# Second tile's queries moved up, norm moved behind the scores, and ten gather places from the 13th gather on

## The chip, the cores and the metric

The kernel runs on one core of a Trainium2 chip. The metric is the device time of one execution in microseconds; the time of a kernel is the median of its runs. A profiled execution gives the trace. Engines: TensorE (PE), VectorE (DVE), ScalarE (ACT), GpSimd (POOL), and SyncE (SP), which issues most of the DMA transfers.

## What is computed

The program computes two transformer blocks on 256 tokens of width 1024, all in float32. The change lies in the second half of the first block, a feed-forward layer of 16384 single-neuron experts (PEER):

```python
h = h + hybrid_mixer(rmsnorm(h, norm_mix), ...)
h = h + peer_ffn(rmsnorm(h, norm_ffn), peer_wq, peer_subkeys, peer_u, peer_v)

def peer_ffn(h, wq, subkeys, u, v):
    q = (hf @ wq).reshape(T, 8, 2, 128)                   # 8 heads, two half queries
    s = einsum('thpd,hpnd->thpn', q, subkeys)             # 128 keys for each half
    s1, i1 = top_k(s[:, :, 0], 16); s2, i2 = top_k(s[:, :, 1], 16)
    cand = s1[..., :, None] + s2[..., None, :]            # 256 pairs
    top_s, pos = top_k(cand, 16)                          # 16 experts for a token and head
    w = softmax(top_s)
    coef = w * gelu(einsum('cd,chkd->chk', x, u[idx]))
    return einsum('chk,chkd->cd', coef, v[idx])
```

The rmsnorm divides each token by its root mean square and multiplies each column by a gain. A query and a score are linear in their token, so a factor of a token may be applied before the queries or to the scores. The second block (a delta-rule mixer and experts of 2 x 1024) follows.

## The kernel before

The 256 tokens are two tiles (t = 0, 1) of 128 partitions. `merge_and_peer` ends the mixer and does the PEER layer. Five engine programs run side by side; each engine works strictly in the order in which its calls are written, and semaphores (`wait_ge`) tie them. Nothing else sets an order.

**End of the mixer.** `up(t, c, half)` (PE L1136) and `merge` (DVE L1799, L1802) build the merged branches, `project` (PE L1147) multiplies by w_out, `residual` (DVE L1807) adds to h. `squares` (ACT L1509), `mean` (DVE), `root` (ACT L1514) and the reciprocal (DVE L1818) give the inverse root mean square of each token; `scale` (DVE L1821) writes the scaled token, `transposes` (PE L1156) turn it, `evacuate` (ACT L1519 and DVE L1826, four blocks each) bring it to hT with the gains.

**Queries and keys.** There are 8 heads. Heads 0 and 1 have their weights in `first_wq`, heads 2 to 7 come through a ring of four pieces (`late_ring`, SP L83) and are split in a high and a low part (`split_high`, ACT L1549; `split_low`, DVE L1837), as hT is (`parts_high`, ACT L1543; `parts_low`, DVE L1831). `first_queries` (PE L1167) and `first_scores` (L1174) do tile 0 of heads 0 and 1, `second_queries` (L1181) and `second_scores` (L1189) tile 1 of them; `queries` (L1199) and `scores` (L1212) do the other heads for both tiles at once. The keep functions of ACT copy the results out of PSUM (queries L1524, L1533, L1553; scores L1528, L1537, L1557). A unit u is a tile and a head, 16 in all, tile 0 first. `first_level`, `pairs`, `places` and `experts_of` (DVE, from L1847 on) choose the unit's 16 experts, `place_numbers` (PE L1246) and `keep_numbers` (DVE L1894) bring their numbers into the order of the gathers, `weights` (ACT L1562), `share_out`, `place_shares` (PE L1253) and `keep_shares` do the softmax.

**Gathers.** GpSimd issues 256 indirect gathers (L1109), 16 for a unit. Gather n, counted from 0, brings 128 rows of 8 KB (an expert's u and v), so 1 MB. `dots` (DVE L1921) multiplies u with the tokens, `coefficients` (ACT L1642 gelu, L1649 two or four diagonals) and `picks` (PE L1224) add the weighted v. They go in quads j of four gathers; up to quad 11 in two groups of two. When a group's picks are done its places are free (`slot_free`), and a later gather may be issued into them. Sixteen places of 1 MB exist; many hold something else at first. Places 0 to 5 are free early, 6 after the projection of tile 1, 7 and 8 hold `first_wq` and are free after `second_queries` of heads 0 and 1, 9 is hT. The table `phases` says which places take turns from which gather on:

```python
phases = [(0, range(AFTER_OUT - 1)), (12, range(AFTER_OUT)), (26, range(EARLY)), (96, ...), (144, ...)]
```

with AFTER_OUT = 7 and EARLY = 10: six places, seven from gather 12, ten from 26, twelve from 96, eleven from 144. For a place that held something else the issue waits: `out_ps` 4 for place 6, `q0_ps` 3 for 7, `q0_ps` 4 and `h_low` 2 for 8 and 9.

SP copies the normalised tokens of tile 0 to the order of the gathers (16 DMAs, L1066), which the first dot needs.

Of the kernel before, what the change touches and what calls it, by code (L numbers as in the profile page):

```python
# [13 lines left out]
ALU = mybir.AluOpType  # L14
# [898 lines left out]
def merge_and_peer(T):  # L913
# [19 lines left out]
    for j in range(QUADS):  # L933
# [44 lines left out]
    phases = [(0, range(AFTER_OUT - 1)), (12, range(AFTER_OUT)), (26, range(EARLY)), (96, [i for i in range(OVER_ROWS) if i not in (AT_ONCE, AT_ONCE + 1)]),  # L978
              (144, [i for i in range(len(slot_of)) if i not in (AT_ONCE, AT_ONCE + 1, EARLY - 1, EARLY, EARLY + 1)])]
# [7 lines left out]
    for n in range(PICKS):  # L987
# [20 lines left out]
    squares_done, mean_done, root_done, scaled, bank_ready, h_act, h_dve, h_high, h_low = (sem(f"ffn_{n}") for n in (  # L1008
        "squares", "mean", "root", "scaled", "bank_ready", "h_act", "h_dve", "h_high", "h_low"))
# [41 lines left out]
    with nc.Block() as block:  # L1051
        @block.sync
        def _(sync):
# [6 lines left out]
            sync.wait_ge(up_ps, 5)  # L1060
            for u in range(4, 6):
                late_ring.issue(sync, u - 4, T.stream1(G_WQ + u))
            sync.wait_ge(row_ready, 1)
            for g in range(4):
                for k in range(4):
                    sync.dma_start(rows_at[0][32 * k:32 * (k + 1), g, :], token_rows[0][32 * g:32 * (g + 1), :]).then_inc(first_rows, 16)  # L1066
            sync.wait_ge(up_ps, 6)
# [59 lines left out]
        def _(pe):  # L1127
# [24 lines left out]
            def transposes(t):  # L1152
                for b in range(2):
                    pe.wait_ge(scaled, 2 * t + b + 1)
                    for k in range(4):
                        last = nc.tensor.transpose(ps[:, 2 * t + b, k * P:(k + 1) * P], xs[:, t, (4 * b + k) * P:(4 * b + k + 1) * P],  # L1156
                                                   ident[:, :])
                    last.then_inc(bank_ready, 1)
# [19 lines left out]
            def second_queries(hd):  # L1178
                for c in range(2):
# [5 lines left out]
            def second_scores(hd):  # L1185
                pe.wait_ge(q_sb, (4, 6)[hd])
# [18 lines left out]
            def scores(hd):  # L1205
                pe.wait_ge(q_sb, {2: 3, 3: 5}.get(hd, hd + 3))
# [178 lines left out]
            project(0)  # L1385
            up(1, 0, 0)
            up(1, 0, 1)
            transposes(0)
# [24 lines left out]
            for j in range(2, QUADS):  # L1413
                if j == 2:
                    picks(2, slice(0, 1))
                    transposes(1)
                    place_shares(1)
                    picks(2, slice(1, 2))
                elif j == 3:
                    picks(3, slice(0, 1))  # L1420
                    pe.wait_ge(h_low, 2)
                    queries(4)
                    queries(5)
                    picks(3, slice(1, 2))
# [13 lines left out]
                if j == 4:  # L1438
                    scores(2)
                    queries(6)  # L1440
                    second_queries(0)
                if j == 5:
                    scores(3)
                if j == 6:
                    second_scores(0)
                    second_queries(1)
# [49 lines left out]
        def _(act):  # L1496
# [38 lines left out]
            def second_keep_scores(hd):  # L1535
                act.wait_ge(sc_ps, hd + 5)
                nc.scalar.activation(sc[:, 1, 2 * hd:2 * hd + 2, :], ps[:, 2 + hd, 0:2 * NKEYS].rearrange("p (c k) -> p c k", c=2),  # L1537
                                     ACT.Copy).then_inc(sc_sb, 1)
# [16 lines left out]
            def keep_scores(hd):  # L1555
                act.wait_ge(sc_ps, hd + 1 if hd < 4 else hd + 3)
                nc.scalar.activation(sc[:, :, 2 * hd:2 * hd + 2, :], ps[:, 2 + hd % 2, :].rearrange("p (t c k) -> p t c k", t=NT, c=2),  # L1557
                                     ACT.Copy).then_inc(sc_sb, 1)
# [100 lines left out]
            squares(0, 0)  # L1659
            squares(0, 1)  # L1660
            root(0)
            evacuate(0)
# [7 lines left out]
            squares(1, 0)  # L1670
            coefficients(2)
            squares(1, 1)
            root(1)
            act.wait_ge(out_ps, 2 * NT)
# [1500 lines left out]
```

## Time and profile before

| | us |
|---|---|
| median of 3 runs | 2092.22 (2092.11 to 2095.01) |
| profiled execution | 2084.8 |
| its span (first to last instruction) | 2083.0 |
| PE busy | 1383.6 (66%) |
| DVE busy | 753.2 (36%) |
| ACT busy | 421.1 (20%) |
| POOL busy | 414.6 (20%) |
| DMA, mean of the whole | 355 GB/s |

Times in the text are microseconds from the start of the span. The gathers run from 250.7 to about 932. The profile splits the span in 40 slices of 52 us and gives the DMA's share for each; the same can be had for any stretch. A share slightly above 1 is rounding of the packets' times and means a full DMA.

### The profile page before, as it was taken

The numbers are of one execution on the slowest core, as the hardware profiler recorded it, in microseconds if no ns is written. First come the engines' busy times: TensorE is split into PE (matmuls) and PEld (weight loads), VectorE is DVE, ScalarE is ACT, GpSimd is POOL, SyncE is SP. The second block draws the span as 40 slices with busy tenths as digits, with TensorE's granted clock in tenths as the row PEclk, the third lists the DMA queues.
The fourth block names the chain that finished last, engine by engine and source line by source line (L and its number), as shares of the span: only waits on it lengthen the run. The fifth ranks groups of instructions, "written<-read, shape, count | busy, mean of one in ns | idle before, by whom it ended". The sixth has DMA issues, their size and how long they took to land. (4 is left out here: it accounts for less than half of the span.)

```text
span 2083.0 us, 24370 instructions
## 1 busy us (share of the span) xinstructions
PE 1383.6 (66%) x9429; PEld 614.3 (29%) x9429; DVE 753.2 (36%) x1687; ACT 421.1 (20%) x1005; POOL 414.6 (20%) x353
## 2 busy tenths in 40 slices
PE   7998967655443333358988876666666676666665
PEld 7887934322010000016887211011111110111111
DVE  4565466677777767646653100000000000000001
ACT  4456132222223211216532100000000000000001
POOL 0141134444444444424540000000000000000000
PEclk9999988877656655579999988777788777777877
DMA  7534579999999999996226899999999999999997
GB/s 269 179 126 166 165 283 380 419 421 420 398 419 421 420 420 420 420 385 251 79 86 247 356 420 420 420 421 420 420 421 420 420 421 421 420 420 420 420 420 324
DMA packets 110711, 739.43 MB, mean 355 GB/s; under 512 B 13472, under 2 KB 14752, under 8 KB 26656
## 3 DMA queue, kind: packets, MB, share of 16 engines
q1 hardware_dynamic: 73472, 469.71, 55.8%
q0 software_dynamic: 36864, 268.45, 31.3%
q8 instruction: 58, 0.95, 0.2%
q14 instruction: 29, 0.24, 0.0%
q10 hardware_dynamic: 288, 0.08, 0.0%
HBM read 735.05 MB, written 1.05 MB: 353 GB/s over the span
## 5 line engine op out<-in xcount | busy, mean ns | idle before, releaser
L2807 PE MATMUL ps<-arena,xe 128*32 128x512 f32 x2016 | 367.4, 821 | 185.1 <-DMA arena<-in_experts_in 184.3
L1224 PE MATMUL ps<-arena 128*32 128x512 f32 x768 | 245.6, 948 | 292.7 <-ACT arena L1649 292.7
L2987 DVE TENSOR_TENSOR low<-low,ps 128x512 f32<-128x512 f32 x16 | 11.0, 688 | 878.3 <-PE ps L2807 878.3
L1109 POOL DMA_INDIRECT arena<-in_peer,arena x192 | 223.9, 1166 | 387.2 <-PE ps L1224 270.9
L1921 DVE CUSTOM_DVE_ANT_0 arena<-arena 128x1024 f32<-128x1024 f32 x192 | 233.1, 1224 | 118.2 <-DMA arena<-in_peer,arena 117.6
L2835 PE MATMUL ps<-arena,hT 128*32 128x512 f32 x1024 | 161.5, 733 | 82.0 <-DMA arena<-in_experts_down 70.9
L3019 POOL TENSOR_TENSOR low<-h,hT 128x512 f32<-128x512 f32 x2 | 2.5, 1264 | 993.2 <-DVE h L3003 993.2
L2807 PEld LDWEIGHTS ps<-arena,xe 128*32 128x32 f32 x2016 | 47.3, 123 | 492.9 <-DMA arena<-in_experts_in 464.2
L1224 PEld LDWEIGHTS ps<-arena 128*32 128x32 f32 x768 | 41.0, 147 | 418.2 <-ACT arena L1649 339.6
L1642 ACT ACTIVATE arena<-arena 128x4 f32<-128x4 f32 (+2 forms) x81 | 16.6, 204 | 467.0 <-DVE arena L1921 466.9
L1224 PE MATMUL ps<-peer_slot,arena 128*32 128x512 f32 x100 | 81.1, 960 | 16.6 <-ACT arena L1649 16.6
L2835 PEld LDWEIGHTS ps<-arena,hT 128*32 128x32 f32 x1024 | 25.5, 121 | 201.1 <-DMA arena<-in_experts_down 160.8
L1224 PE MATMUL ps<-ring,arena 128*32 128x512 f32 x112 | 60.2, 1040 | 35.8 <-ACT arena L1649 35.8
L2824 PE MATMUL ps<-low,og 128*128 128x512 f32 x128 | 71.9, 689 | 11.5 <-ACT low L2898 11.5
L2898 ACT ACTIVATE low<-ps 128x512 f32<-128x512 f32 x32 | 19.1, 597 | 262.8 <-PE ps L2835 262.8
L2895 ACT ACTIVATE hT<-ps 128x512 f32<-128x512 f32 x16 | 9.5, 596 | 303.4 <-PE ps L2814 303.4
L2890 ACT ACTIVATE low<-ps 128x512 f32<-128x512 f32 x16 | 9.6, 597 | 283.8 <-PE ps L2807 283.8
L1279 PE MATMUL ps<-first_h_parts,first_w_parts 128*128 128x256 f32 x480 | 63.6, 291 | 2.5 <-ACT first_h_parts L1579 1.9
L1649 ACT ACTIVATE arena<-arena 128x32 f32<-128x32 f32 x256 | 63.1, 311 | 7.9 <-DVE arena L1909 0.4
L1279 PEld LDWEIGHTS ps<-first_h_parts,first_w_parts 128*128 128x128 f32 x480 | 60.1, 196 | 7.6 <-issue 3.5
L1117 POOL TENSOR_TENSOR first_w_parts<-arena,first_w_parts 128x512 fp32r<-128x512 f32 x36 | 49.3, 1385 | 61.7 <-ACT first_w_parts L1586 61.1
L513 PE MATMUL ps<-first_h_parts,first_w_parts 128*128 128x256 f32 x384 | 50.1, 287 | 2.5 <-POOL first_w_parts L481 2.2
(481 smaller groups left out, 2009.1 us busy)
## 6 DMA issues: line engine op xcount, KB each, us to landing
arena<-in_experts_in SPq DMA_DIRECT2D x252, 1024.0 KB, 26.9
arena<-in_experts_down SPq DMA_DIRECT2D x128, 1024.0 KB, 26.9
ring<-in_stream SPq DMA_DIRECT2D x38, 512.0 KB, 4.4
arena<-in_stream SPq DMA_DIRECT2D x32, 512.0 KB, 4.1
arena<-in_stream SPq DMA_DIRECT2D x14, 1024.0 KB, 8.2
first_out_w<-in_stream SPq DMA_DIRECT2D x8, 512.0 KB, 7.3
arena<-in_peer,arena POOLq DMA_INDIRECT x192, 15.0
arena<-arena SPq DMA_DIRECT2D x16, 128.0 KB, 2.4
```

The costliest lines, as they stand in the source:

```text
L513: last = nc.tensor.matmul(ps[:, 7, (u % 2) * S:(u % 2 + 1) * S], w[:, k, :], T.parts[:, x, k, :], start=(k == 0 and m == 0), stop=(k == KB ...
L1109: nc.gpsimd.indirect_dma_start(slot(n), None, A["peer"], bass.IndirectOffsetOnAxis(ap=idx[:, u % 3, k:k + 1], axis=0)).then_inc(landed[pla ...
L1117: nc.gpsimd.tensor_tensor(low, half_raw(u, hk), high.bitcast(F32), ALU.subtract).then_inc(f_low, 1)
L1224: last = nc.tensor.matmul(ps[32 * g:32 * (g + 1), 4 + 2 * t + half, :], diag[:, n % DIAGS, :], slot(n)[:, D + half * BANK:D + (half + 1) * ...
L1279: last = nc.tensor.matmul(ps[:, n % 4, half * S:(half + 1) * S], w[:, k, :], T.parts[:, x, k, :], start=(k == 0 and m == 0), stop=(k == KB ...
L1642: nc.scalar.activation(act_out[:, u % 2, some], act_in[:, u % 2, some], ACT.Gelu).then_inc(gelu_done, 1)
L1649: nc.scalar.activation(diag[:, n % DIAGS, :], shares[:, u % 2, n % TOPK, :], ACT.Copy, scale=act_out[:, u % 2, n % TOPK:n % TOPK + 1]).the ...
L1921: nc.vector.tensor_tensor_reduce(slot(n)[:, 0:D], slot(n)[:, 0:D], rows_at[n // FIRST][:, n % G, :], 1.0, 0.0, ALU.mult, ALU.add, act_in[: ...
L2807: last = nc.tensor.matmul(ps[32 * j:32 * (j + 1), 4 + r // KB, :], xe[:, k, :], w[:, j * BANK:(j + 1) * BANK], start=(k == 0), stop=(k == ...
L2824: last = nc.tensor.matmul(ps[:, 2 * t + half, :], og[:, t * P:(t + 1) * P], yb[:, half * BANK:(half + 1) * BANK], start=opening, stop=clos ...
L2835: last = nc.tensor.matmul(ps[32 * j:32 * (j + 1), 6 + half, :], hidT[:, i, 32 * j:32 * (j + 1)], w[:, j, :], start=(i == 0), stop=(i == 3) ...
L2898: nc.scalar.activation(yb[:, half * BANK:(half + 1) * BANK], ps[:, 6 + half, :], ACT.Copy).then_inc(y_ready, 1)
```

## The change

Five things change together, all in `merge_and_peer`.

1. The transposes read h itself and not the scaled token; `scale` is gone, `invert` keeps only the reciprocal. The factor of the token is applied where ACT copies the scores out of PSUM, for heads 2 to 7 with one copy for each tile instead of one for both.
2. For tile 0 the first half of the transposes goes into the projection, and `up(1, 0, ...)` and `merge(1, 0)` behind the first two heads.
3. SP issues the 16 token copies ahead of weight pieces 4 and 5 instead of behind them.
4. For tile 1 the order of ACT, DVE and PE around quads 1 to 4 is rewritten; `second_queries(0)` and `(1)` follow the transposes in quads 2 and 3, and not in quads 4 and 6.
5. `phases`: ten places from gather 12, twelve from 102, eleven from 138.

```diff
-    phases = [(0, range(AFTER_OUT - 1)), (12, range(AFTER_OUT)), (26, range(EARLY)), (96, [i for i in range(OVER_ROWS) if i not in (AT_ONCE, AT_ONCE + 1)]),
-              (144, [i for i in range(len(slot_of)) if i not in (AT_ONCE, AT_ONCE + 1, EARLY - 1, EARLY, EARLY + 1)])]
+    phases = [(0, range(AFTER_OUT - 1)), (12, range(EARLY)), (102, [i for i in range(OVER_ROWS) if i not in (AT_ONCE, AT_ONCE + 1)]),
+              (138, [i for i in range(len(slot_of)) if i not in (AT_ONCE, AT_ONCE + 1, EARLY - 1, EARLY, EARLY + 1)])]
@@ transposes (PE)
-                    pe.wait_ge(scaled, 2 * t + b + 1)
+                    pe.wait_ge(res_done, 2 * t + b + 1)
@@ second_queries (PE)
+                pe.wait_ge(h_act, 8)
+                pe.wait_ge(h_dve, 8)
@@ PE, tile 0
-            project(0)
-            up(1, 0, 0)
-            up(1, 0, 1)
-            transposes(0)
+            project(0, range(6))
+            transposes(0, range(1))
+            project(0, range(6, 8))
+            transposes(0, range(1, 2))
...
+            up(1, 0, 0)
+            up(1, 0, 1)
             up(1, 1, 0)
+            place_numbers(0)
             up(1, 1, 1)
             up(1, 2, 0)
-            place_numbers(0)
@@ first_keep_scores (ACT; the other two copies of scores likewise)
+                act.wait_ge(rstd, 1)
-                                     ACT.Copy).then_inc(sc_sb, 1)
+                                     ACT.Copy, scale=ssq[:, 10:11]).then_inc(sc_sb, 1)
@@ DVE, tile 1
-            residual(1, 1)
-            mean(1)
-            keep_numbers(1)
-            scale(1)
-            split_low(4)
-            dots(4)
-            share_out(1)
-            evacuate(1)
-            split_low(5)
-            parts_low(0)
-            dots(5)
-            parts_low(1)
+            dots(4)
+            keep_numbers(1)
+            residual(1, 1)
+            dots(5)
+            evacuate(1)
+            parts_low(0)
+            mean(1)
+            share_out(1)
+            dots(6)
+            invert(1)
+            parts_low(1)
+            split_low(4)
+            dots(7)
+            keep_shares(1)
+            split_low(5)
```

**ScalarE, from the coefficients of gathers 4 and 5 to those of 10 and 11.** L1642 is the gelu of a group and L1649 its diagonals, L1509 the squares, L1514 the root, L1562 the softmax's exp, L1549 and L1543 the high parts of weights and of hT. Before:

```order
L1509 ACTIVATE arena,ffn_ss<-h 128x512
L1514 ACT_TABLE_LOAD
L1514 ACTIVATE ffn_ss<-ffn_ss 128x1
L1549 ACTIVATE first_w_parts<-ring1 128x1024
L1642 ACT_TABLE_LOAD
L1642 ACTIVATE arena<-arena 128x2
L1649 ACTIVATE arena<-arena 128x32 x2
L1562 ACT_TABLE_LOAD
L1562 ACTIVATE arena<-arena 128x16
L1543 ACTIVATE first_h_parts<-hT 128x8x128
L1549 ACTIVATE first_w_parts<-ring1 128x1024
```

The first gelu here is that of gathers 6 and 7: squares, root and a weight's split stand ahead of it.

The same place now (gelu L1655, diagonals L1662, squares L1517, root L1522, exp L1575, split of weights L1558, of hT L1552, evacuation L1527, copy of the second tile's queries L1542), from the diagonals of gathers 6 and 7 on:

```order
L1662 ACTIVATE arena<-arena 128x32 x2
L1575 ACT_TABLE_LOAD
L1575 ACTIVATE arena<-arena 128x16
L1655 ACT_TABLE_LOAD
L1655 ACTIVATE arena<-arena 128x2
L1662 ACTIVATE arena<-arena 128x32 x2
L1552 ACTIVATE first_h_parts<-hT 128x8x128
L1517 ACTIVATE arena,ffn_ss<-h 128x512 x2
L1655 ACTIVATE arena<-arena 128x2
L1662 ACTIVATE arena<-arena 128x32 x2
L1527 ACTIVATE hT<-ps,gains 128x128 x4
L1522 ACT_TABLE_LOAD
```

The coefficients of 6 and 7 come first, then exp, those of 8 and 9, the squares, those of 10 and 11, and the root behind them. And on, up to the coefficients of gathers 12 and 13 (second gelu row's L1662) and 14 and 15:

```order
L1542 ACTIVATE arena<-ps 128x2x128
L1552 ACTIVATE first_h_parts<-hT 128x8x128
L1558 ACTIVATE first_w_parts<-ring1 128x1024
L1655 ACT_TABLE_LOAD
L1655 ACTIVATE arena<-arena 128x2
L1662 ACTIVATE arena<-arena 128x32 x2
L1542 ACTIVATE arena<-ps 128x2x128
L1558 ACTIVATE first_w_parts<-ring1 128x1024
L1655 ACTIVATE arena<-arena 128x2
L1662 ACTIVATE arena<-arena 128x32 x2
```

The copies of the second tile's queries (L1542) now stand ahead of both groups' coefficients.

**TensorE, from the second tile's transposes (L1156) on.** Picks are L1224 before and L1226 now, shares L1253 and L1255, queries of heads 2 and on L1199 and L1201. Before:

```order
L1156 MATMUL ps<-ident,arena 128x128 x8
L1253 MATMUL ps<-peer_small 32x16 x4
L1224 MATMUL ps<-arena 32x512 x8
L1199 MATMUL ps<-first_h_parts,first_w_parts 128x256 x48
L1224 MATMUL ps<-arena 32x512
```

Now:

```order
L1156 MATMUL ps<-ident,h 128x128 x8
L1226 MATMUL ps<-arena 32x512 x4
L1183 MATMUL ps<-hT,arena 128x128 x16
L1226 MATMUL ps<-arena 32x512 x4
L1255 MATMUL ps<-peer_small 32x16 x4
L1183 MATMUL ps<-hT,arena 128x128 x16
L1226 MATMUL ps<-arena 32x512
```

The second tile's queries of heads 0 and 1 (L1183) stand between the picks of quads 2 and 3, where before there were picks alone and then the queries of head 2.

## Rows read from the trace of the kernel before

**Rows 1.** The page's second part: DMA share in 40 slices.
```profile
DMA  7534579999999999996226899999999999999997
```

**Rows 2.** Windows: length, busy us of each engine, clock, DMA share, GB/s.
```profile
283.00:292.00 9.00, 3.89 (x10) 0.69 (x12) 4.75 (x9) 8.33 (x14) 1.88 (x2) 0.66 0.22 67
...
302.00:311.00 9.00, 7.73 (x35) 3.27 (x36) 6.20 (x10) 2.12 (x9) 3.25 (x3) 0.77 0.25 75
...
341.00:346.00 5.00, 5.00 (x26) 2.75 (x23) 4.93 (x8) 0.74 (x3) 1.91 (x2) 0.73 0.33 103
346.00:534.00 188.00, 107.43 (x650) 52.52 (x652) 136.75 (x334) 50.01 (x136) 84.66 (x72) 0.78 1.01 417
534.00:538.00 4.00, 1.03 (x8) 0.00 (x0) 3.97 (x9) 0.00 (x0) 2.05 (x3) 0.90 0.60 199
```

**Rows 3.** GpSimd: its waits from 250 to 372, then gathers 11, 12, 16.
```profile
POOL arena L1109 <- PE ps L1224: 60.6, 11, 11.4
...
276.80 1.39 POOL L1109 DMA_INDIRECT arena<-in_peer,arena  x1 [0.30 <-issue]
289.62 0.94 POOL L1109 DMA_INDIRECT arena<-in_peer,arena  x1 [11.44 <-PE ps L1224]
...
307.14 1.86 POOL L1109 DMA_INDIRECT arena<-in_peer,arena  x1 [10.29 <-PE ps L1224]
```

**Rows 4.** Timeline around the holes: start, length, engine, line, idle before and releaser.
```profile
276.14 1.23 DVE L1921 CUSTOM_DVE_ANT_0 arena<-arena 128x1024 f32<-128x1024 f32 x1 [1.15 <-DMA arena<-in_peer,arena]
...
279.81 0.68 DVE L1807 TENSOR_TENSOR h<-h,ps 128x512 f32<-128x512 f32 x1
...
282.67 1.04 ACT L1549 ACTIVATE first_w_parts<-ring 128x1024 fp32r<-128x1024 f32 x1
...
283.73 1.28 ACT L1642 ACT_TABLE_LOAD   x1
...
285.85 3.49 PE L1224 MATMUL ps<-arena 128*32 128x512 f32 x8 [5.64 <-ACT arena L1649]
...
294.32 1.84 PE L1156 MATMUL ps<-ident,arena 128*128 128x128 f32 x8
...
302.79 3.55 PE L1224 MATMUL ps<-arena 128*32 128x512 f32 x8 [6.45 <-ACT arena L1649]
...
334.19 3.73 PE L1181 MATMUL ps<-hT,arena 128*128 128x128 f32 x32
...
340.05 3.46 PE L1224 MATMUL ps<-arena 128*32 128x512 f32 x8 [2.14 <-ACT arena L1649]
```

**Rows 5.** Timeline of the first tile, from its residual to the first gather.
```profile
229.54 0.69 DVE L1807 TENSOR_TENSOR h<-h,ps 128x512 f32<-128x512 f32 x1 [6.46 <-PE ps L1147]
...
232.92 1.04 PE L1156 MATMUL ps<-ident,arena 128*128 128x128 f32 x8
...
234.84 3.81 PE L1167 MATMUL ps<-hT,arena 128*128 128x128 f32 x32 [0.89 <-ACT hT L1519]
...
240.35 0.49 DVE L1847 MAX8 arena<-arena 128x8 f32<-128x128 f32 x2 [2.20 <-ACT arena L1528]
...
250.73 1.15 POOL L1109 DMA_INDIRECT arena<-in_peer,arena  x1 [73.94 <-DVE arena L1894]
```

**Rows 6.** SyncE's issues: weight pieces (L83) and token copies (L1066).
```profile
233.11 0.80 SPq L83 DMA_DIRECT2D ring<-in_stream  x2
...
236.58 10.95 SPq L1066 DMA_DIRECT2D arena<-arena  x16
...
248.26 0.81 SPq L83 DMA_DIRECT2D ring<-in_stream  x2
```

**Rows 7.** Prices: picks at full clock, head 2's first keys, unit 2's numbers.
```profile
306.82 1.91 PE L1224 MATMUL ps<-arena 128*32 128x512 f32 x8 [0.48 <-ACT arena L1649]
...
332.15 0.49 DVE L1847 MAX8 arena<-arena 128x8 f32<-128x128 f32 x2 [6.07 <-ACT arena L1557]
...
349.04 0.17 DVE L1894 CAST arena<-ps 128x16 uint32<-128x16 f32 x1
```

More of the change, by code:

```diff
@@ L1007, in merge_and_peer @@
         "no_ready", "no_ps", "share_ready", "share_ps", "shares", "row_ps", "row_kept", "first_rows"))
-    squares_done, mean_done, root_done, scaled, bank_ready, h_act, h_dve, h_high, h_low = (sem(f"ffn_{n}") for n in (
-        "squares", "mean", "root", "scaled", "bank_ready", "h_act", "h_dve", "h_high", "h_low"))
+    squares_done, mean_done, root_done, rstd, bank_ready, h_act, h_dve, h_high, h_low = (sem(f"ffn_{n}") for n in (
+        "squares", "mean", "root", "rstd", "bank_ready", "h_act", "h_dve", "h_high", "h_low"))
     q0_ps, w_high, w_low, unit_done, q_sb = (sem(f"ffn_{n}") for n in ("q0_ps", "w_high", "w_low", "unit_done", "q_sb"))
@@ L1556, in keep_scores @@
                 act.wait_ge(sc_ps, hd + 1 if hd < 4 else hd + 3)
-                nc.scalar.activation(sc[:, :, 2 * hd:2 * hd + 2, :], ps[:, 2 + hd % 2, :].rearrange("p (t c k) -> p t c k", t=NT, c=2),
-                                     ACT.Copy).then_inc(sc_sb, 1)
+                if hd == 2:
+                    act.wait_ge(rstd, 2)
+                for t in range(NT):
+                    last = nc.scalar.activation(sc[:, t, 2 * hd:2 * hd + 2, :], ps[:, 2 + hd % 2, 2 * t * NKEYS:2 * (t + 1) * NKEYS].rearrange("p (c k) -> p c k", c=2),
+                                                ACT.Copy, scale=ssq[:, 10 + t:11 + t])
+                last.then_inc(sc_sb, 1)
             def weights(u):
@@ L1814, in mean, with invert @@
                                                ALU.mult, ALU.add).then_inc(mean_done, 1)
-            def scale(t):
+            def invert(t):
                 dve.wait_ge(root_done, t + 1)
-                link(nc.vector.reciprocal(ssq[:, 10 + t:11 + t], ssq[:, 8 + t:9 + t]))
-                for b in range(2):
-                    cols = slice(b * BANK, (b + 1) * BANK)
-                    nc.vector.tensor_scalar(xs[:, t, cols], h[:, t, cols], ssq[:, 10 + t:11 + t], None, ALU.mult).then_inc(scaled, 1)
+                nc.vector.reciprocal(ssq[:, 10 + t:11 + t], ssq[:, 8 + t:9 + t]).then_inc(rstd, 1)
+                dve.wait_ge(rstd, t + 1)
             def evacuate(t):
@@ L2052, in _ @@
             residual(0, 1)
+            evacuate(0)
             mean(0)
-            scale(0)
-            evacuate(0)
+            invert(0)
             dve.wait_ge(peer_consts, 32)
-            dve.wait_ge(h_act, 4)
-            dve.wait_ge(h_dve, 4)
             token_row(0)
-            merge(1, 0)
             nc.vector.reduce_sum(stacked[:, :], ident[:, :].rearrange("p (g r) -> p r g", g=4), AX.X)
@@ L2066, in _ @@
             share_out(0)
-            for c in range(1, 4):
+            for c in range(4):
                 merge(1, c)
```

76 lines of the change are left out of this document (40 added, 36 removed).

## The prediction

> **What bounds the kernel now.** I read the page first: its DMA row [rows 1] stands at nine tenths or more from the eighth slice on, and again over the last twenty slices. Two stretches of the program move data as fast as the chip gives it; the first (252 to 928 us) is the 256 gathers, 1 MB each. The windows of equal state [rows 2] show a share of 1.01 where nothing stops them (346 to 534 us at 417 GB/s: 2.5 us for a gather), and four holes. Against a share of 1.00 they are 9 x 0.78 = 7.0 us at 283 to 292, 9 x 0.75 = 6.8 at 302 to 311, 5 x 0.67 = 3.4 at 341 to 346 and 4 x 0.40 = 1.6 at 534 to 538: together 18.8 us. Everything after the last gather waits for it, so the time of the whole moves with the sum of the holes and with the start of the stream, and with nothing else in this stretch. In the undisturbed stretch TensorE is busy for 57%, VectorE for 73 and ScalarE for 27: none of them sets the pace.
>
> Then the queue of the gathers [rows 3]: GpSimd waited 60.6 us for the matmuls of L1224 (they free a place), and its long waits end at 289.62 and 307.14, each after 10 us or more, with the holes in front. So a hole is a late slot: landing, dot (DVE L1921), gelu and two diagonals (ACT), eight matmul halves (PE), then the next gather.
>
> Who is late at each hole [rows 4]. First: gathers 6 and 7 have landed by 276.14 (the dot of 7 stood waiting for it), yet their matmuls start at 285.85, because ScalarE did the second tile's norm (squares for DVE's residual at 279.81, root) and a weight split (282.67) ahead of their coefficients. Second: the matmuls at 302.79 stand behind the transposes of 294.32, their evacuation and the wait of DVE for it. Third: the matmuls at 340.05 stand behind a head's queries (334.19, 3.73 us).
>
> **Start, worked out.** Before, residual (229.54) to first keys (240.35) holds squares, mean, root, two scalings and the transposes [rows 5]. Now the transposes read h at once: the first four go into the projection (0.52 us, half of the 1.04 of the row at 232.92), so the projection ends at 230.0; residual to 230.9; the other four to 231.5; queries 3.81 us to 235.3 instead of 238.65; their evacuation, scores and the scaled copy follow as before, so the first keys start at 237.1, 3.3 us earlier. The rstd is there by 233.9: squares (0.8), mean, root and reciprocal (1.0 together) run beside the queries. From keys to first gather 10.4 us as before, so 247.5 instead of 250.73; TensorE's three halves of `up` put ahead of the numbers end at 246.8, inside that.
>
> But the stream of the weights moves too [rows 6]. Before, SP issued two 512 KB pieces at 233.11, into an idle DMA, then the 16 row copies (10.95 us), then two pieces at 248.26. Now the row copies come first (235.4 to 246.4), and all four pieces, 2 MB, go out from 246.5 to 249.8, at the door of the gathers. That is 1 MB more, 2.5 us. Position of the stream: before, 9 MB (two pieces, eight gathers) stood between 248.26 and gather 7's landing at 276.14; they are 22.5 us of transfer, and 5.4 of delay and gaps. Now 10 MB from 246.5: 25.0 + 5.4 gives 276.9, 0.8 late, less what of the gaps closes now that the gathers are issued at once behind the pieces. **The head start is worth 0** (bounds: 3.2 gained if the pieces fit into gaps, 1 lost). DVE is at its merges until 257.6 anyway, since TensorE's last half of `up` ends at 256.3.
>
> **First hole.** Up to gather 11 all is as before, within 0.3 us. ScalarE goes from the coefficients of gathers 4 and 5 straight to those of 6 and 7: dots done at 277.4, diagonals 278.3; TensorE, behind the numbers of unit 1 (280.3), picks at 280.5 and frees them by 282.4 (1.91 us at 2.4 GHz [rows 7]). Gather 12 is issued at 282.6 and not 289.62, before the queue is dry (284). **Hole gone: 7.0 us.** What is next: gathers 8 and 9 are picked at 283.5 to 285.4, transposes to 286.5, and gather 11, the last landed (286.1 by the pace from 276.14), has its dot at 287.4, coefficients 288.2, picks 290.2. So 12 to 17 are issued on time.
>
> **Second hole, turned into another.** Ten places take turns from gather 12, so 18 and 19 need no freed place: 18 the second tile's projection, 19 the first head's queries (q0_ps 3). 20 and 21 need the second head's queries (q0_ps 4). TensorE does the first head's at 290.2 to 293.9; 19 goes out at 294.3. The DMA is then fed until 284.2 + 8 x 2.5 = 304.2. Chain to gather 20, on ScalarE: root (before 290.9), copy of the queries 0.4, h's high part 1.05, weight split 1.04, gelu table back 1.28, coefficients 0.8: 298.5. On TensorE: picks 3.55 at 1.2 GHz, since it has stood for 4.6 us (the row at 302.79 is such a case), 302.1; shares 0.3; queries 3.7: 306.1. Gather 20 is issued at 306.5 and moves from 307.9: **a hole of 3.7 us**, instead of 6.8. The new waits of TensorE (h_act, h_dve, q_sb) end before and cost nothing; if DVE were 3 us later at 300 they still would not.
>
> **Third hole.** Then, in order: query copy and split to 307.6, coefficients 308.4, picks 310.4, two query units (3.0 each) 316.4, split 318.2, coefficients of 16 and 17 at 319.0, picks 321 (322.6 at 1.2 GHz), head 2's scores and two scaled copies 323 to 324.5. The queue holds 20 to 25 and two pieces of weights: 307.9 + 6 x 2.5 + 2.5 = 325.4, so 26 comes in time; 28 to 31 follow at 326 to 334 and fill until 342. Gather 32 needs unit 2's numbers: before, 16.9 us from its first keys (332.15) to the numbers (349.04), now plus one split (1.2): 324 + 18.1 = 342.1, moving at 343.5. **Hole 1.5 us** (0 to 4) instead of 3.4. From there ten places as before, and the engines are some 8 us earlier but the DMA 12 us: 1 us of small gaps allowed. The keeping of scores is now two copies with a scale for six heads: 0.4 us each on an engine that is a fifth busy.
>
> **Fourth.** The hole at 534 stands where the turn shrinks and a place comes round after 8 gathers while picks go in fours. The later phase (102) has two such gathers, 108 and 109, five behind the end of their quad as before: 1.6 stays. At 145 the distance is six: one gather more of slack, nothing.
>
> **Sum.** Holes before 18.8; after 3.7 + 1.5 + 1.0 + 1.6 = 7.8. Gain 11.0 us, start 0. Profiled execution: span 2083.0 (2084.8 with what lies around it), now 2072. It lies 7 us under the median of the runs, 2092.2, in which the same 11.0 come off: **2081**.
>
> The Trainium skill, ScalarE: Activation LUTs, "What ACT_TABLE_LOAD costs", gives each change of table set a drain of 1.38 us beside the load of 1.28. The trace shows the load alone: 283.73 + 1.28 ends at 285.01, and the coefficients' matmuls begin at 285.85 after a gelu and two copies of 0.8 us in all; no drain fits. By the page two changes (exp to gelu, root to gelu) would lie ahead of gathers 8 and 20, of which the second counts: a hole of 5.1, total 2082.
>
> **Rivals.**
> *Late second head (chance 0.17).* The same mechanism, but TensorE at 1.2 GHz in more of the chain: picks of 10 and 11 at 3.5, both heads' queries at 7.4. For it: 285.85, 302.79 and 340.05 are all at that clock after 2 to 6 us of standing. Against: 306.82 and 334.19 are back at 2.4. One head's queries slow and the picks before them: + 1.6 + 3.7 us, and a split further behind: holes 13 to 15, gain 4 to 6, 2087.
> *The start counts (0.08).* Pieces fit beside the first gathers and the third hole closes: 3 more from the start, 2 from holes: 2076.
> *Slower than before (0.06).* Gathers 20 and 21 stop GpSimd, and with it 22 to 25, whose places are free: the turn of ten makes the stream wait for the second head where a turn of seven would have gone on. With both heads at 1.2 GHz: queries to 299.3, ScalarE 303.9, picks 307.4, queries 315.2, a hole of 12.5 us instead of 3.7; the same delay of some 10 us runs through queries 4 and 5 to gather 26 and on to 32, where the next hole is then 10 or more, and the pieces' 2.5 us at the start are lost. It decides above 19 us of holes: 26, time 2099.
> *It does not arrive (0.04).* The gathers end 11 us earlier, but the later stages give part back: 2092. Against: the loads of the next stage are released by the last gathers; no row shows another clock.
> The forecast has the rest, 0.65, with its own range 2077 to 2085.
>
> **How the numbers follow.** 0.2% is 4.2 us, about what a measurement of this kernel can tell from no change. Faster: 0.65 + 0.08 + two thirds of the late second head (0.11) = 0.84, of which 0.04 goes off for what I have not seen, half to each side: 0.80. Within: 0.06 + 0.04 + 0.02 = 0.12. Slower: 0.06 + 0.02 = 0.08. The range takes in the late second head and the early start: 2075 to 2089.
>
> **What would show it.** Gather 12 issued within a microsecond of 283, no hole at 284. A hole that ends at GpSimd's wait for the second head's queries near 307 (gather 20); 19 issued near 294. First gather at 247.5 but its dots not before 257. Holes in all near 8 us, and the last gather landing 11 us earlier. Wrong would be: a first hole that is still there (ScalarE or the residual late), gather 20 later than 312, or a stream at less than 420 GB/s between the holes.

## The result and the profile after

The changed kernel takes 2079.49 us (median of 5 runs, 2075.34 to 2083.99) against 2092.22 (median of 5 runs, 2091.01 to 2096.52) of the kernel before: a ratio of 0.9934, 95% interval 0.9915 to 0.9953, or 12.7 us less (9.8 to 17.8). The forecast was 2081, range 2075 to 2089. The time is right; the sum behind it is not in all its terms, and this section and the experiments show which.

The profiled execution took 2075.34 us, its span is 2073.6. Beside [rows 1], the page's row of the DMA's share in 40 slices of 52 us:

```profile
DMA  7544599999999999986306899999999999999997
```

Before, the nines begin in the seventh slice (the prediction says the eighth); now they begin in the sixth, 260 to 312 us, where the first two holes lay, and the gathers' row of nines ends a slice sooner. The windows that answer to [rows 2] (length, busy us of PE, PE's weight loads, DVE, ACT and POOL, granted clock of TensorE as a share of 2.4 GHz, DMA share, GB/s):

```profile
283.00:292.00 9.00, 5.62 (x30) 1.85 (x28) 7.09 (x15) 5.62 (x17) 4.25 (x4) 1.00 0.95 366
292.00:302.00 10.00, 5.50 (x40) 3.92 (x38) 7.10 (x15) 5.64 (x9) 3.96 (x4) 0.92 1.00 414
302.00:311.00 9.00, 6.78 (x52) 4.49 (x50) 2.84 (x5) 1.95 (x5) 2.31 (x2) 0.88 0.76 292
311.00:341.00 30.00, 24.04 (x140) 15.24 (x138) 19.99 (x52) 7.76 (x20) 14.13 (x11) 0.89 1.00 410
341.00:346.00 5.00, 2.58 (x24) 1.43 (x22) 4.90 (x13) 4.59 (x8) 1.12 (x2) 1.00 0.97 396
346.00:534.00 188.00, 104.50 (x616) 46.24 (x612) 144.81 (x351) 47.02 (x136) 87.84 (x74) 0.77 1.01 418
...
541.00:547.00 6.00, 3.52 (x28) 0.66 (x20) 3.35 (x6) 2.48 (x3) 3.32 (x3) 0.86 0.79 294
```

A share of 0.22 at 283 has become 0.95, 0.25 at 302 has become 0.76, 0.33 at 341 has become 0.97. The undisturbed stretch moves 418 GB/s, before it was 417. What made the difference, GpSimd's gathers 12, 19, 20 and 32 (start, length, idle before and its releaser; beside [rows 3]):

```profile
284.84 0.94 POOL L1109 DMA_INDIRECT arena<-in_peer,arena  x1 [4.04 <-PE ps L1226]
...
297.51 0.93 POOL L1109 DMA_INDIRECT arena<-in_peer,arena  x1 [0.30 <-issue]
...
308.39 0.94 POOL L1109 DMA_INDIRECT arena<-in_peer,arena  x1 [9.94 <-PE ps L1183]
...
344.58 0.94 POOL L1109 DMA_INDIRECT arena<-in_peer,arena  x1 [4.37 <-DVE arena L1907]
```

Gather 12 goes out at 284.84 and not at 289.62, and the one long wait left, 9.94 us, ends with the second head's queries (L1183). Around it, on TensorE and ScalarE (as [rows 4]):

```profile
282.67 1.89 PE L1226 MATMUL ps<-arena 128*32 128x512 f32 x8
...
287.73 1.09 PE L1156 MATMUL ps<-ident,h 128*128 128x128 f32 x8
...
290.87 1.91 PE L1226 MATMUL ps<-arena 128*32 128x512 f32 x8 [2.05 <-ACT arena L1662]
...
292.71 3.84 PE L1183 MATMUL ps<-hT,arena 128*128 128x128 f32 x32
...
298.88 1.28 ACT L1655 ACT_TABLE_LOAD   x1
...
300.17 0.20 ACT L1655 ACTIVATE arena<-arena 128x2 f32<-128x2 f32 x1
...
301.05 2.77 PE L1226 MATMUL ps<-arena 128*32 128x512 f32 x6 [4.50 <-ACT arena L1662]
...
304.28 3.84 PE L1183 MATMUL ps<-hT,arena 128*128 128x128 f32 x32
```

The picks of 6 and 7 at 282.67, the transposes at 287.73, the first head's queries at 292.71, then 4.50 us in which TensorE waits for the coefficients of 12 and 13, and the second head's at 304.28.

**Landmarks.** Span times of two executions can't be laid over each other: the subkeys' load, an instruction of SP ahead of all edits, stands at 200.35 us before and 203.57 after. So I count from it, in us, worked out from the start times of single rows. A hole is a run of slices of 1 us with a DMA share under 0.8; the sum is what they lack. "Rest" is the stretch from the last gather's dot to SP's load of the router weights, which no edit touches; from there to the end all lie within 970.3 and 973.4.

| execution | gather 0 | gather 7's dot | gather 12 | gather 20 | gather 32 | last dot | sum of holes | rest | span |
|---|---|---|---|---|---|---|---|---|---|
| before | 50.4 | 75.8 | 89.3 | 112.7 | 155.8 | 734.4 | 18.6 | 177.5 | 2083.0 |
| before_again | 50.4 | 77.7 | 91.3 | 112.9 | 158.0 | 735.7 | 19.2 | 179.0 | 2091.2 |
| before_c | 50.4 | 78.0 | 91.4 | 113.8 | 156.7 | 735.4 | 18.4 | 187.2 | 2096.8 |
| before_d | 50.4 | 77.1 | 90.7 | 114.0 | 157.4 | 735.3 | 19.4 | 186.8 | 2096.4 |
| after | 46.7 | 75.2 | 81.3 | 104.8 | 141.0 | 718.1 | 3.4 | 180.9 | 2073.6 |
| again | 46.7 | 75.7 | 81.8 | 108.1 | 142.6 | 719.8 | 6.1 | 183.2 | 2078.5 |
| after_c | 46.7 | 76.2 | 82.4 | 107.3 | 141.9 | 720.3 | 6.3 | 185.5 | 2078.6 |
| after_d | 46.7 | 74.8 | 80.8 | 107.2 | 141.8 | 718.8 | 5.3 | 180.6 | 2071.5 |

The first four rows are the kernel before, the last four the changed one. The last dot moves from 735.2 to 719.3 on the mean of four: **16.0 us, not 11**. Of these 1.7 us are there at gather 7's dot (77.2 to 75.5). The stretch from that dot to the last one is the steadiest measure, 657.4 to 658.6 us before and 642.9 to 644.1 in the changed kernel: it leaves out what an execution gained or lost ahead of the holes, and is 14.3 us shorter on the mean.

### The profile page after: what moved, and what is told of

It reads as the page before. It is cut to its first block and busy times, and to the rows that moved or that the text cites. A ratio compares the mean times of both kernels' runs of the same rounds, so it can differ in the third digit from the quotient of the medians.

```text
span 2073.6 us, 24377 instructions
## 1 busy us (share of the span) xinstructions
PE 1384.3 (67%) x9429; PEld 618.2 (30%) x9429; DVE 753.0 (36%) x1683; ACT 422.4 (20%) x1011; POOL 416.0 (20%) x353
## 5 line engine op out<-in xcount | busy, mean ns | idle before, releaser
L1226 PE MATMUL ps<-arena 128*32 128x512 f32 x768 | 241.9, 954 | 270.0 <-ACT arena L1662 269.8
L1226 PEld LDWEIGHTS ps<-arena 128*32 128x32 f32 x768 | 40.7, 147 | 386.7 <-ACT arena L1662 310.4
L1655 ACT ACTIVATE arena<-arena 128x4 f32<-128x4 f32 (+2 forms) x81 | 16.5, 204 | 455.5 <-DVE arena L1934 455.5
L1226 PE MATMUL ps<-peer_slot,arena 128*32 128x512 f32 x100 | 81.8, 968 | 18.5 <-ACT arena L1662 18.5
L1226 PE MATMUL ps<-ring,arena 128*32 128x512 f32 x108 | 53.9, 998 | 44.5 <-ACT arena L1662 44.5
L1662 ACT ACTIVATE arena<-arena 128x32 f32<-128x32 f32 x256 | 63.1, 311 | 7.9 <-DVE arena L1922 0.4
```

Source lines behind the costliest of these rows:

```text
L1226: last = nc.tensor.matmul(ps[32 * g:32 * (g + 1), 4 + 2 * t + half, :], diag[:, n % DIAGS, :], slot(n)[:, D + half * BANK:D + (half + 1) * ...
L1662: nc.scalar.activation(diag[:, n % DIAGS, :], shares[:, u % 2, n % TOPK, :], ACT.Copy, scale=act_out[:, u % 2, n % TOPK:n % TOPK + 1]).the ...
```

## Experiments

Times of the runs are medians; a ratio is against the kernel before on the same chip. All rows for comparison are in the table above and in this one:

| execution | gather 7's dot | gather 12 | gather 20 | gather 32 | last dot | sum of holes | rest | time | ratio (95%) |
|---|---|---|---|---|---|---|---|---|---|
| again | 75.7 | 81.8 | 108.1 | 142.6 | 719.8 | 6.1 | 183.2 | 2078.51 | 0.9922 (0.9892 to 0.9951) |
| seven | 74.3 | 80.4 | 103.1 | 146.0 | 724.6 | 7.7 | 182.6 | 2085.38 | 0.9969 (0.9952 to 0.9986) |
| squares_first | 76.8 | 89.1 | 110.7 | 148.3 | 725.2 | 8.6 | 180.9 | 2080.42 | 0.9936 (0.9911 to 0.9960) |
| start_only | 74.6 | 88.0 | 110.4 | 153.4 | 733.4 | 19.0 | 182.5 | 2094.36 | 1.0004 (0.9989 to 1.0020) |
| short_pieces | 75.0 | 81.1 | 104.7 | 140.8 | 717.7 | 3.3 | 182.0 | 2072.5 (one run) | |
| coefs_first | 74.3 | 80.4 | 99.6 | 134.1 | 712.7 | 1.0 | 185.5 | 2070.62 | 0.9876 (0.9859 to 0.9893) |
| both | 75.0 | 81.3 | 103.1 | 139.2 | 715.4 | 0.2 | 183.8 | 2071.25 | 0.9877 (0.9858 to 0.9897) |

### The changed kernel once more

> The changed kernel once more, for the spread of its stages. Theory (holes in the stream of gathers): the stretch of the gathers is again 16 us shorter than before, counted from the loads of the subkeys to the dot of gather 255, and the holes of the stream sum to 4 to 6 us; what differs between two profiles before that stretch and behind it (3.2 and 3.4 us in the two profiles at hand) is chance of the clock and changes sign from run to run. Rival (the later stages give part back): the 3.4 us between the last dot and the router's loads are there again, with the same sign.

The changed kernel as it is. The second hole is 4.4 us, not 2.3, and the reason stands on TensorE and GpSimd:

```profile
290.26 3.35 PE L1226 MATMUL ps<-arena 128*32 128x512 f32 x8 [2.05 <-ACT arena L1662]
...
293.55 4.04 PE L1183 MATMUL ps<-hT,arena 128*128 128x128 f32 x32
...
305.73 4.74 PE L1183 MATMUL ps<-hT,arena 128*128 128x128 f32 x32
...
310.75 0.94 POOL L1109 DMA_INDIRECT arena<-in_peer,arena  x1 [11.28 <-PE ps L1183]
```

The same eight matmul halves that took 1.91 us in the first execution take 3.35, and the two heads' queries 0.2 and 0.9 more. The window shows a granted clock of 0.58 here, so most of it is at 1.2 GHz; in the first execution these halves had 1.00:

```profile
290.00:293.60 3.60, 3.34 (x9) 0.57 (x9) 3.24 (x9) 2.72 (x7) 0.15 (x1) 0.58 1.01 414
```

That is the rival "late second head" in half measure, and it changes from one execution of the same program to the next: the hole is 2.3, 4.4, 3.1 and 4.0 us in the four. The second head's queries take 4.7 to 4.9 us in three of them and 3.84 in the first alone, so the execution shown with the result is the mildest.

### The turns of before

```diff
-    phases = [(0, range(AFTER_OUT - 1)), (12, range(EARLY)), (102, ...), (138, ...)]
+    phases = [(0, range(AFTER_OUT - 1)), (12, range(AFTER_OUT)), (26, range(EARLY)), (96, ...), (144, ...)]
```

> The changed kernel with the table of turns of the kernel before (seven places from gather 12, ten from 26). Theory: gathers 19 to 21 then wait for the picks of 12 to 14, which end near 303, and 22 and 23 for those of 15 and 16, of which 16 comes only behind head 2's queries at 322: the queue runs dry once near 305 to 308 as now (2 to 3 us) and again for 8 to 12 us before 325; together 10 us slower than the changed kernel. Rival (the order of ScalarE and of the queries does it all, the turns nothing): within 1 us of the changed kernel.

The last dot is 5.3 us later than the changed kernel's mean, 6.5 by the stretch from gather 7's dot, and the time is 6.9 us longer than that of the changed kernel on the same chip. So the new turns are worth 5 to 7 us beside the new order, rather more than half of the 10 that were expected. The edit puts back the later turns too, but nearly all of the loss is there by gather 32. With seven places the gathers 19, 21 and 23 wait in turn for picks:

```profile
304.35 0.94 POOL L1109 DMA_INDIRECT arena<-in_peer,arena  x1 [7.77 <-PE ps L1226]
305.59 0.94 POOL L1109 DMA_INDIRECT arena<-in_peer,arena  x1 [0.30 <-issue]
313.45 1.30 POOL L1109 DMA_INDIRECT arena<-in_peer,arena  x1 [6.93 <-PE ps L1226]
315.06 0.94 POOL L1109 DMA_INDIRECT peer_slot<-in_peer,arena  x1 [0.30 <-issue]
323.68 0.94 POOL L1109 DMA_INDIRECT arena<-in_peer,arena  x1 [7.69 <-PE ps L1226]
```

One hole has become three smaller ones (1.6, 2.5 and 2.3 us), spread over 20 us. The rest of the loss is not in holes of this size: gather 20 is even earlier than with ten places (103.1), gather 32 is 4.2 us later than the mean 141.8. Gather 12 goes out at 80.4 and the first hole stays closed, so that one does not need the turns.

### The squares ahead of the coefficients of gathers 6 and 7

```diff
             coefficients(2)
+            squares(1, 0)
+            squares(1, 1)
             coefficients(3)
             weights(1)
             coefficients(4)
             act.wait_ge(out_ps, 2 * NT)
             parts_high(0)
-            squares(1, 0)
-            squares(1, 1)
             coefficients(5)
```

> The changed kernel with ScalarE's squares of tile 1 ahead of the coefficients of gathers 6 and 7, as before. Theory: the squares wait for DVE's second residual (now behind the dots of 8 and 9, 285.7), so the picks of 6 and 7 move from 282.7 to 288 and gather 12 from 284.8 to 290: a hole of 4 to 5 us opens at 287 and everything behind it moves by as much. Rival (later waits absorb it, since gather 20 waits for the queries anyway): gather 20 is late by less than 1 us and the hole before it shrinks from 2.3 us to nothing, net 2 us.

ScalarE (squares, then the gelu of gathers 6 and 7), TensorE and GpSimd (gather 12), and the window of the first hole:

```profile
284.28 0.63 ACT L1517 ACTIVATE arena<-h 128x512 f32<-128x512 f32 x1 [11.41 <-DVE h L1822]
...
284.91 0.19 ACT L1655 ACTIVATE arena<-arena 128x2 f32<-128x2 f32 x1
...
285.71 3.62 PE L1226 MATMUL ps<-arena 128*32 128x512 f32 x8 [4.29 <-ACT arena L1662]
...
289.62 0.94 POOL L1109 DMA_INDIRECT arena<-in_peer,arena  x1 [12.14 <-PE ps L1226]
...
283.00:292.00 9.00, 6.06 (x17) 1.16 (x18) 3.71 (x8) 6.63 (x16) 1.87 (x2) 0.62 0.20 62
```

The squares moved ahead on ScalarE wait 11.41 us for the residual. Counted from the subkeys' load, the picks go back from 79.1 to 85.2 and to 3.62 us, and the hole at 283 is back with a share of 0.20 (7.2 us; 4 to 5 were expected). So with all else in place this order alone opens the first hole. It is not a copy of before: there the residual came earlier (279.81) and root, table loads and a weight's split made up the delay; here DVE does the residual behind the dots of gathers 8 and 9. The last dot is 5.9 us later and not 7.2, and 1.3 of that stand at gather 7's dot already, so the edit is worth 4.6 to 5.9. Gather 12 is 7.5 us later than the mean of the changed kernel, gather 20 only 3.8, and the second hole is gone (0.3 us), as the rival had it in part: while the queue stands still at the first hole, the second head's queries catch up. In the time it is 1.9 us, less than the runs can tell.

### The start alone

Items 1 to 3 of the change put into the kernel before; order of tile 1 and turns as they were. (Its diff is that of items 1 to 3 in the change, with `invert(1)` where `scale(1)` stood.)

> The kernel before with the start alone: transposes that read h, the norm behind the scores, tile 0's order, the token copies ahead of weight pieces 4 and 5. Tile 1's order and the turns are those of before. Theory: the first gather is issued 3.7 us earlier counted from the subkeys' loads, gather 7 lands 0.6 earlier, the four holes stay (19 us), the time is 0 to 1 us under the kernel before. Rival (the start counts): gather 7 lands 3 us earlier and the whole is 3 us faster.

Gather 0 is 3.7 us earlier, the four holes are there undiminished (19.0), the last dot lies at 733.4 against 735.2, the mean of four of before. So the start is worth 1.8 us at the end of the gathers, on one execution against four that spread over 1.3, and nothing that the runs can tell. GpSimd's rows show a delay for gather 5, in this kernel, then before:

```profile
256.59 0.93 POOL L1109 DMA_INDIRECT arena<-in_peer,arena  x1 [2.64 <-PE ps L1136]
```

```profile
257.16 0.94 POOL L1109 DMA_INDIRECT arena<-in_peer,arena  x1 [0.30 <-issue]
```

Gather 5 goes to a place that TensorE's `up` for tile 1 (L1136) still reads, and that work now stands behind the first heads' queries. It waits 2.64 us that it did not wait before. Counted from the subkeys' load gather 4 is 3.6 us earlier (52.0 against 55.6) and gather 5 only 1.2 (55.6 against 56.8). But this wait is not what keeps the gain small, for the DMA is full all the while, in this kernel:

```profile
247.00:252.00 5.00, 5.00 (x51) 4.97 (x52) 2.80 (x9) 0.00 (x0) 3.37 (x4) 1.00 1.01 323
252.00:257.00 5.00, 5.00 (x52) 4.85 (x51) 1.77 (x5) 0.00 (x0) 1.94 (x3) 1.00 1.01 409
257.00:262.00 5.00, 5.00 (x48) 4.88 (x46) 4.33 (x13) 0.74 (x3) 0.52 (x1) 1.00 1.02 422
262.00:276.00 14.00, 12.48 (x83) 7.78 (x83) 12.05 (x37) 2.09 (x8) 6.07 (x5) 1.00 1.01 417
```

None of these windows has a share under 1, so a gather issued sooner would only have queued. What is left to take the rest of the 3.7 us is the content of the queue: four weight pieces stand ahead of the gathers, where before there were two. The next run asks what they cost.

### Two short pieces of weights

```diff
             for u in range(4, 6):
-                late_ring.issue(sync, u - 4, T.stream1(G_WQ + u))
+                sync.dma_start(late_ring.piece(u - 4)[:, 0:64], T.stream1(G_WQ + u)[:, 0:64]).then_inc(late_ring.loaded[u - 4], 16)
```

Of pieces 4 and 5 only 64 of 1024 columns are loaded, so 15/16 of 1 MB is left out and head 2 (this one alone, not heads 2 to 7) computes with what lies there.

> The changed kernel with weight pieces 4 and 5 loaded only in their first 64 of 1024 columns, so that 1 MB of the 2 MB at the door of the gathers is left out (the queries of heads 2 to 7 then use stale weights; the work is the same). Theory (the moved pieces cost 2.5 us of the stream and eat the head start): gather 7 lands 2 to 2.5 us earlier, counted from the subkeys' loads (73 instead of 75.2), and the last dot comes 2 us earlier than in the changed kernel (716 to 718 instead of 718 to 720). Rival (the pieces fit into gaps): both where they are, within 0.5 us.

With this megabyte gone gather 7's dot stands at 75.0 (75.5 on the mean of the four executions with it, 74.8 to 76.2) and gather 12 at 81.1 (81.6 on the mean). So leaving it out gains about 0.5 us, within the spread, and not 2.5. The last dot is at 717.7 against 719.3, but the holes behind the start, which differ by chance, are 2.0 us shorter too. The windows of the start tell why, in this kernel:

```profile
247.00:252.00 5.00, 5.00 (x47) 5.00 (x47) 2.66 (x9) 0.00 (x0) 3.76 (x4) 1.00 0.65 195
252.00:257.00 5.00, 5.00 (x52) 4.85 (x51) 2.13 (x6) 0.00 (x0) 1.94 (x3) 1.00 1.02 419
```

and in the changed kernel, 3 us later on the clock of its span:

```profile
250.00:255.00 5.00, 5.00 (x47) 5.00 (x46) 2.60 (x8) 0.00 (x0) 3.82 (x4) 1.00 0.97 338
255.00:260.00 5.00, 5.00 (x52) 4.85 (x51) 2.20 (x6) 0.00 (x0) 1.95 (x3) 1.00 1.00 394
```

In the first 5 us the pieces raise what is moved from 195 to 338 GB/s: 0.7 MB of the 1 MB moves in room that the first gathers leave. The rival of this run (the pieces fit into gaps) holds.

### The coefficients of 12 and 13 right behind the root

```diff
             root(1)
+            coefficients(6)
             second_keep_queries(0)
             parts_high(1)
             split_high(4)
-            coefficients(6)
```

> The changed kernel with ScalarE's coefficients of gathers 12 and 13 directly behind the root, ahead of the first query copy, the high part of hT and the weight split. Theory (TensorE stands for 4.5 us behind those three, which makes gather 20 late and throws its clock to 1.2 GHz): TensorE goes from the first head's queries into the picks with no pause, the second head's queries end 5 to 6 us earlier, gather 20 is issued near 99 to 100 us from the subkeys' loads instead of 105 to 108, and the hole of 2.3 to 4.4 us is gone. Last dot 2 to 4 us earlier. Rival (h_low 2, two steps behind the moved copies, becomes what gather 20 waits for): gather 20 at 102 or later, hole 0 to 1.

If the second hole is the chain copy, parts, split, table, coefficients on ScalarE and then slow picks on TensorE, this removes it. TensorE and GpSimd:

```profile
292.88 3.88 PE L1183 MATMUL ps<-hT,arena 128*128 128x128 f32 x32
...
296.68 1.48 PE L1226 MATMUL ps<-arena 128*32 128x512 f32 x6
...
298.57 3.84 PE L1183 MATMUL ps<-hT,arena 128*128 128x128 f32 x32
...
302.68 0.99 POOL L1109 DMA_INDIRECT arena<-in_peer,arena  x1 [4.25 <-PE ps L1183]
```

The picks follow the first head's queries with no wait; six of them take 1.48 us where they took 2.77 after 4.50 us of standing. Gather 20 is 7.3 us earlier than the changed kernel's mean (99.6 against 106.9), the hole is 0.2 us, the last dot 6.6 us earlier (712.7 against 719.3), of which 1.2 are there at gather 7's dot, ahead of the edit: 5.4 are the edit's, more than the 2 to 4 expected. This is the second hole's cause, shown. The time is 2070.62 us, 0.9876 of before (0.9859 to 0.9893). It beats the kernel before. Against the changed kernel the traces say the same; the two were not timed on one chip, and the intervals of their ratios just touch (`again` has 0.9892 to 0.9951), so how much of the 5.4 us arrives in the time is not shown.

### The same with other turns at the end

```diff
-              (102, [i for i in range(OVER_ROWS) if i not in (AT_ONCE, AT_ONCE + 1)]),
-              (138, [...])]
+              (102, [0, 1, 2, 3, 10, 11, 12, 13, 6, 7, 8, 9]),
+              (138, [0, 1, 2, 3, 12, 13, 14, 15, 6, 7, 8])]
```

on top of the kernel before this one: the places that join the turn come ahead of those that were taken last.

> coefs_first with the later turns in another order: the new places 10 to 13 come before 6 to 9 in the turn from gather 102, and 12 to 15 before 6 to 8 in the turn from 138, so that no place comes round after 8 gathers. Theory (the hole at 543 is the short turn): that hole of 1.2 to 1.5 us goes too; holes sum to under 1.5 us, last dot 4 to 6 us before that of the changed kernel, the time 2075. Rival (the hole at 543 is the wait for the last scores, sc_sb 10): it stays or grows, since place 10 is now asked for four gathers earlier.

The fourth hole goes: a window of 6 us over it held 0.79 in `coefs_first` and holds 1.02 here.

```profile
536.00:542.00 6.00, 3.64 (x24) 0.70 (x16) 2.57 (x7) 2.48 (x3) 3.79 (x4) 0.77 0.79 289
```

```profile
538.00:544.00 6.00, 4.75 (x32) 1.03 (x24) 4.09 (x11) 2.76 (x6) 0.94 (x1) 0.75 1.02 419
```

But the last dot is at 715.4, 2.7 later than without it, and the time is the same within what can be told. The loss lies ahead of the edit: counted from the subkeys' load the picks of 10 and 11 start 2.4 us later (88.7 against 86.3) behind gathers that landed late, and the first head's queries take 4.96 us instead of 3.88. From gather 32 to the last dot this execution is the shortest, 576.2 us against 577.0 to 578.6 in the five that have the hole. Whether the last hole's 0.8 us arrive in the time stays open; it is too small for these runs.

### The kernel before again, and two more of each

> The kernel before once more, for the spread of its stages. Theory: the first dot to the last as in the first profile (holes 18 to 19 us, last dot 734 us from the subkeys' loads, within 1), and the stretch from the last dot to the router's loads longer than the 177.5 us of the first profile, by chance of the clock, as it was 180.9 to 183.2 in the others. Rival (the change itself costs 3 us there): 177.5 again, within 1.

> The kernel before once more, for the stretch from the last dot to the router loads, which no edit touches: 177.5 and 179.0 us in two executions of it, 180.9 and 183.2 in two of the changed kernel. Chance: one more of before lies anywhere from 177 to 185. The gathers' earlier end is partly given back there (the rival that does not arrive): below 180. Subkeys load to last dot: 734 to 736 by both.

> The changed kernel once more. Chance: last dot to router loads anywhere from 177 to 185. Given back: above 180.5. Subkeys load to last dot: 718 to 720 by both, with a hole of 2 to 4.5 us near 307.

> As the other look at the kernel before: by chance 177 to 185 us from the last dot to the router loads, given back below 180.

> As the other look at the changed kernel: by chance 177 to 185 us from the last dot to the router loads, given back above 180.5.

After the first executions it looked as if the later stages gave 3 us of the gathers' gain back: rest 177.5 and 179.0 before, 180.9 to 183.2 after. Two more of each give no sign of it: the means of four are 182.6 before (177.5 to 187.2) and 182.6 after (180.6 to 185.5). `before_again`, with 179.0, fits neither of its two expectations (clearly longer than 177.5, or within 1 of it). The band that I expected by chance, 177 to 185, was too narrow (187.2, 186.8 and 185.5 lie outside), and with such a spread four executions of each cannot exclude a loss of 2 or 3 us; that the whole gain is given back they do exclude. What sets the rest stands in its window, from the last dot to the router's loads, in before, then in before_c (the column of the granted clock is the third from the end):

```profile
934.77:1112.31 177.54, 160.30 (x1964) 138.94 (x1962) 107.47 (x205) 85.19 (x177) 76.07 (x75) 0.96 0.32 128
```

```profile
937.45:1124.60 187.15, 169.69 (x1964) 147.87 (x1962) 107.15 (x205) 85.16 (x177) 75.86 (x75) 0.91 0.31 122
```

The same 1964 matmuls keep TensorE busy for 160.3 us in one and 169.7 in the other, while the other engines' busy times agree within 0.4 us. The granted clock is 0.96 and 0.91 (0.95 and 0.91 in before_again and before_d, which took 179.0 and 186.8). A clock short of full by 0.04 over 177.5 us and by 0.09 over 187.2 is 7.1 and 16.8 us lost (an estimate from these shares): the whole difference of 9.7.

## Why the prediction was right, and where it was not

**First hole, right.** Forecast: gather 12 at 282.6, no hole. Measured: 284.84 on the span's clock, less the 3.2 us by which this execution's subkeys' load is later: 281.6. That is a microsecond before the stated one (283, within 1). The DMA share is 0.95. Three runs place the cause: items 1 to 3 alone leave the hole at 7.2 us (`start_only`), without item 5 it stays closed (`seven`), and with all five in place and the squares ahead of the coefficients it is 7.2 us again (`squares_first`). So item 4 closes it, and ScalarE's order is the part of it that cannot be missing.

**Second hole, right in place and size.** Forecast 3.7 us, gather 20 at 306.5, 19 at 294.3. Measured 308.39 and 297.51 less 3.2: 305.2 and 294.3; hole 2.3, and 2.3 to 4.4 over four executions, 3.5 on the mean. That 19 met its time is in part luck: it did not wait for the first head's queries but for nothing except its turn behind gathers 16 to 18 (`issue`), of which 16 had waited 2.81 us for picks. `coefs_first` shows the cause of this hole. Of its steps one was off for the first execution: the picks took 3.2 us (301.05 to 304.28), forecast 3.55. The forecast weighed a drain beside the table load of 1.28 us that the Trainium skill, ScalarE: Activation LUTs, "What ACT_TABLE_LOAD costs", would add. The load of 298.88 ends at 300.16 and the gelu starts at 300.17, so here is no drain, and the 5.1 us by the page's rule did not come.

**Third hole, wrong.** Forecast 1.5 us (0 to 4), measured none: share 0.97 at 341 to 346. Gather 32 was foreseen at 342.1 and went out at 344.58 less 3.2, 341.4, so the engines were as forecast. The step that failed is the content of the queue, "20 to 25 and two pieces of weights", to which 28 to 31 are added but no further piece. SP issued four pieces of 512 KB there:

```profile
314.24 23.29 SPq L83 DMA_DIRECT2D ring<-in_stream  x4
```

Twelve gathers and four pieces are 14 MB, 35 us from 309.5 on, which lasts to 344.5; by the prediction's own sum 342 becomes 344.5, later than the 343.5 at which it let gather 32 move. So the second megabyte, 2.5 us, covers the hole by this count; no run leaves it out.

**Small gaps, 1.0 us allowed, none seen** in the undisturbed stretch (share 1.01, 418 GB/s). The sign "a stream at less than 420 GB/s" came true with 410 to 418 between the holes, but it was set too high: the kernel before had 417 in this stretch.

**Fourth hole, right in size.** Forecast 1.6, measured 1.2, 1.3, 2.6 and 1.1. But "1.6 stays" rested on the one execution of before that shows 1.3; the other three have 0.4 to 0.5 us of it, so the changed kernel's is longer by some 0.9 on the mean. `both` has none, in one execution.

**Start, too low.** Forecast 0, with bounds of 3.2 gained and 1 lost; 1.8 at the last dot by `start_only`, 1.7 at gather 7's dot (77.2 to 75.5 on the means of four). In the forecast's own terms, from SP's issue of the pieces to gather 7's dot: the issue was to move 1.8 us up (248.26 to 246.5) and moved 2.5 (47.9 to 45.4 on the means, counted from the subkeys' load); the megabyte adds 2.5; and "5.4 of delay and gaps" was taken as the same on both sides. It is 6.8 before on the mean of four and 5.1 after. 2.5 gained, 2.5 lost and 1.7 gained give the 1.7. So two terms were mis-sized: the move of the issue, by 0.7, and the gaps, of which 1.7 us close with the pieces in them; that is also why leaving the megabyte out gains only 0.5 (`short_pieces`). The 5.4 came from the fastest of the four executions of before in just this number, gather 7's dot at 75.8 against 77.1 to 78.0. I also let the six gathers go out at once, where gather 5 waits 2.64 us for TensorE's displaced `up`; with the DMA full in that stretch this cost nothing.

**Sum.** Forecast: holes from 18.8 to 7.8, start 0, gain 11.0. Measured on four executions each: holes from 18.9 to 5.3, that is 13.6; start 1.8; 15.4 of the 16.0 at the last dot. The 2.6 us more of holes are the third (1.5) and the small gaps (1.0). The mean span falls by 16.3 us (2091.9 to 2075.6), the medians of the runs by 12.7 and 13.5, with 9.8 to 17.8 as the interval of the first. Taken together, these 24 runs of before and 9 of the changed kernel differ by 13.9 us on the mean (about 11 to 17, an estimate from their spread). So a gain of 11 is at the edge of what the runs allow, and 16 is inside. That 2081 met 2079.5 so closely is partly luck: the first median lies 3 us short of the gain that the traces show, within its spread.

**Rivals.** Late second head: seen as a spread of 2 us within one program, never as its full 13 to 15 us of holes. Start counts: half true, 1.8 of 3 us, and the third hole closed as it said; its 2076, a gain of 16 us, is inside the interval of the runs, and by the traces it was the better description. Slower: gathers 22 to 25 do stand behind 20, but the engines behind were not 10 us late. Does not arrive: refuted by the measured time; a part of 2 or 3 us given back is not excluded, and nothing shows it.

## To carry over

When a stream is the bound, count for each hole every transfer that other queues have put into the same engines, since each megabyte of them is 2.5 us of cover, and ask of a late issue first whether the DMA had run dry: gather 5 waited 2.64 us and no share fell under 1. An engine that mixes small late-needed work (here the squares, then the copies and splits of ScalarE) with the steps that release buffers should do the releasing steps first: the order of a few calls was worth 4.6 to 5.9 us at the first hole and 5.4 at the second. A single profile shows one draw of a granted clock, so compare landmarks inside the stage that was edited, over a few executions, before a theory is made about the stages behind it.

## What I had not expected of the hardware

The granted clock over a stretch in which TensorE is busy nine tenths of the time is not a constant of the program. Over the same 1964 matmuls of the same kernel it was 0.96 and 0.91, and the unedited stage took 177.5 to 187.2 us; this is the larger part of the 13.8 us between the four spans of before. Likewise eight matmul halves behind the same wait of 2.05 us took 1.91 us in one execution of the changed kernel and 3.35 in another. What decides between them no run here shows or controls.
